# Attention stage of a hybrid encoder layer: first heads' probabilities in small buffers, stores issued ahead of the next stage's loads, cache pieces copied behind the exponential

## What is computed

```python
sc = jnp.einsum('blhd,bmhd->bhlm', qc, kb) * scale + bias
sc = jnp.where(valid, sc, -jnp.inf)
p = jax.nn.softmax(sc, axis=-1)
return jnp.einsum('bhlm,bmhd->blhd', p.astype(vb.dtype), vb)
```

## Time and profile before

| what | value |
|---|---|
| runs | 2070.66 us median of 3 (2070.57 to 2071.6) |
| the profiled execution | 2072.05 us; span 2070.3 us |
| mean granted TensorE clock | 0.975 |
| busy: TensorE, VectorE, ScalarE, GpSimd | 1951.8, 742.1, 633.8, 603.2 us |
| attention stage in the trace | from about 613 to about 822 us |

### The profile page before, as it was taken

One profiled execution on the slowest core, in us unless ns is written; L12 is line 12 of the kernel. 1 busy time (PEld: TensorE's weight loads), 2 busy tenths in 40 slices (PEclk: granted clock), 3 DMA queues, 4 the chain that ended last, 5 costly groups with the idle time before them and its releaser, 6 DMA issues. The chain is left out here.

```text
span 2070.3 us, 34075 instructions
## 1 busy us (share of the span) xinstructions
PE 1951.8 (94%) x13954; PEld 1762.3 (85%) x13954; DVE 742.1 (36%) x1467; ACT 633.8 (31%) x1239; POOL 603.2 (29%) x466
## 2 busy tenths in 40 slices
PE   5999999999995888899989999999999999999998
PEld 3999999999993566678789878999999999999996
DVE  4111577211113665465564164222222222222225
ACT  5100222100013665344353244322222222222222
POOL 6111112211122000554244344333333323333323
PEclk7999999999997999899989999999999999999999
DMA  5122222632216321231154322211111111111123
GB/s 136 59 93 86 75 93 90 233 94 90 86 61 199 117 83 38 67 104 46 30 155 145 112 92 92 58 45 41 41 41 41 46 47 41 41 41 41 41 73 151
DMA packets 159271, 169.18 MB, mean 82 GB/s; under 512 B 14187, under 2 KB 130043, under 8 KB 159150
## 3 DMA queue, kind: packets, MB, share of 16 engines
q1 hardware_dynamic: 152814, 141.52, 22.4%
q10 hardware_dynamic: 6336, 25.96, 3.1%
HBM read 126.84 MB, written 40.55 MB: 81 GB/s over the span
## 5 line engine op out<-in xcount | busy, mean ns | idle before, releaser
L2277 DVE TENSOR_TENSOR t_acc<-t_acc,t_B 128x512 f32<-128x512 f32 x252 | 173.4, 688 | 540.7 <-PE t_B L2370 540.7
L116 PE MATMUL i_ps<-x_hi,i_w_lo 128*128 128x384 f32 x1056 | 353.5, 335 | 0.0
L116 PE MATMUL i_ps<-x_hi,i_w_hi 128*128 128x384 f32 x1056 | 353.5, 335 | 0.0
L116 PE MATMUL i_ps<-x_lo,i_w_hi 128*128 128x384 f32 x1056 | 353.3, 335 | 0.0
L2357 PE MATMUL t_B<-t_merged_hi,t_wm_lo 128*128 128x384 f32 x768 | 256.9, 335 | 1.0 <-POOL t_wm_lo L1982 1.0
L2357 PE MATMUL t_B<-t_merged_lo,t_wm_hi 128*128 128x384 f32 x768 | 256.6, 334 | 0.0
L2357 PE MATMUL t_B<-t_merged_hi,t_wm_hi 128*128 128x384 f32 x768 | 256.6, 334 | 0.0
L106 POOL TENSOR_TENSOR i_w_lo<-i_w_raw,i_w_hi 128x1024 fp32r<-128x1024 f32 x44 | 104.9, 2385 | 443.8 <-ACT i_w_hi L101 443.8
L1982 POOL TENSOR_TENSOR t_wm_lo<-t_raw,t_wm_hi 128x1024 fp32r<-128x1024 f32 x49 | 119.2, 2434 | 295.6 <-ACT t_wm_hi L2057 295.6
L116 PEld LDWEIGHTS i_ps<-x_hi,i_w_lo 128*128 128x128 f32 x1056 | 198.8, 188 | 0.0
L116 PEld LDWEIGHTS i_ps<-x_lo,i_w_hi 128*128 128x128 f32 x1056 | 198.7, 188 | 0.0
(11 more groups left out here) (321 smaller groups left out, 3404.4 us busy)
## 6 DMA issues: line engine op xcount, KB each, us to landing
proj<-i_out ACTq DMA_DIRECT2D x44, 576.0 KB, 2.8
i_w_raw<-in_w_in SPq DMA_DIRECT2D x44, 512.0 KB, 3.8
t_raw<-in_w_up SPq DMA_DIRECT2D x32, 512.0 KB, 4.5
t_raw<-in_w_down SPq DMA_DIRECT2D x32, 512.0 KB, 3.6
t_gates<-proj SPq DMA_DIRECT2D x48, 192.0 KB, 2.6
a_k_cache<-in_cache_attn_k SPq DMA_DIRECT2D x8, 1024.0 KB, 5.2
a_v_cache<-in_cache_attn_v SPq DMA_DIRECT2D x8, 1024.0 KB, 5.2
d_c<-proj SPq DMA_DIRECT2D x3, 1536.0 KB, 7.2
```

The costliest lines, as they stand in the source:

```text
L116: last = pe.matmul(out, a[s][:, c, :], b[:, c, tokens], start=k == 0, stop=k == n - 1)
L2277: dve.tensor_tensor(a, a, B[(ND * j + d) % 4][:, :], ALU.add).then_inc(added, 1)
```

## The change

Three edits in `stage_attention`. First, two small buffers of 128 x 128 (`first_pt`) are put behind the exponentials' buffers, and `turned_p(u)` gives them to the units 2, 3, 6 and 7, the only heads of the first block that used `pt[2]` and `pt[3]`. Those buffers' first user is now u = 10, and the wait for the stores moves there. Second, SP issues the two conv loads after the six stores. Third, ScalarE's side jobs stand behind the exponential of their step.

```diff
-        assert late + 8 * KEYS <= env.c_at + 16 * T
+        assert late + 8 * KEYS + 8 * P <= env.c_at + 16 * T
...
+        first_pt = [nc.alloc_sbuf_tensor_at(f"a_first_p_t{i}", [P, P], F32, offset=late + 8 * KEYS + 4 * P * i) for i in range(2)]
...
+        def turned_p(u):
+
+            return first_pt[u % 4 - 2] if u < AH and u % 4 > 1 else pt[u % 4]
...
             sp.wait_ge(pre_d, (NPRE) // 2)
             sp.wait_ge(pre_a, (NPRE + 1) // 2)
-            for a, ts in ((0, TP), (P, 0)):
-                sp.dma_start(env.c0[:, :, a:a + P], env.proj[3 * AW:3 * AW + CONV, ts:ts + P].rearrange(
-                    "(c p) t -> p c t", p=P)).then_inc(env.c_in, 16)
             for h in range(AH):
...
             sp.dma_start(O_["sample_conv"].rearrange("l b w c -> (l b w) c"),
                          tail_out[HIST:ROWS, :]).then_inc(saved, 16)
+            for a, ts in ((0, TP), (P, 0)):
+                sp.dma_start(env.c0[:, :, a:a + P], env.proj[3 * AW:3 * AW + CONV, ts:ts + P].rearrange(
+                    "(c p) t -> p c t", p=P)).then_inc(env.c_in, 16)
             for b in range(2, NB):
...
-                if u == 2:
+                if u == AH + 2:
                     act.wait_ge(saved, 16 * 6)
                 if u >= 4:
                     act.wait_ge(av_made, group(u - 4) + 1)
-                act.activation(pt[u % 4][:, 0:n], TR[:, 0:n], ACT.Copy).then_inc(tr_read, 1)
+                act.activation(turned_p(u)[:, 0:n], TR[:, 0:n], ACT.Copy).then_inc(tr_read, 1)
...
             for st in range(STEPS):
                 if 0 <= st - 3 < NU:
                     turned(st - 3)
-                for j in side_jobs(st):
-                    side_out(j)
                 if st < NU:
...
                                    accum_out=rsum[:, st % SR:st % SR + 1]).then_inc(p_made, 1)
+                for j in side_jobs(st):
+                    side_out(j)
...
-                                         pt[(u + w) % 4][:, i * P:(i + 1) * P], start=i == 0, stop=i == n - 1)
+                                         turned_p(u + w)[:, i * P:(i + 1) * P], start=i == 0, stop=i == n - 1)
```

## The result

The changed kernel took 2056.77 us, the median of four runs (2055.30 to 2059.61), beside 2070.61 for the kernel before (2070.03 to 2071.60): a ratio of 0.9932, interval 0.992 to 0.9943. The forecast was 2053.9 with a range up to 2055.9, so the median lies 0.9 above the range. The profiled execution took 2055.41 with a span of 2053.7; against the 2072.05 of the one profiled before that is -16.64, where the sum said -16.8. Two repeats of the changed kernel gave 2054.26 (ratio 0.9922, 0.9902 to 0.9942) and 2056.34 (0.993, 0.9915 to 0.9945). All its 14 runs lie between 2051.86 and 2061.79 with a median of 2055.9, all 36 runs of the kernel before between 2066.57 and 2076.28 with one of 2071.5.

A forecast was written before the change was run, and what follows sets the result against it. ScalarE's wait at u=2 for the last of six late stores was taken to bound the attention opening. Terms -17.8 and +1.0 sum to -16.8, from the median 2070.66 to 2053.9 us; range 2049.0 to 2055.9.

The forecast's parts named there:

- The stall, -17.8: ScalarE's copy of u=2 no longer waits for the last of six stores and goes on at 633.23: -17.8 us.
- The moved wait, 0: ScalarE at u=10: stores done at 642.2 to 646.0, u=10 due at 649.9 or later, so no cost.
- The small fill just in time, and the hold, +1.0: GpSimd's small bias fill ends at 638.63, in time; its large fill holds VectorE's scaling of u=5: +1.0 us (0.4 to 1.6).
- The third edit, 0: Cache pieces copied behind ScalarE's exponential: no gain or loss, within 1 us either way.
- the rival of 22.6 us: Rival: the third edit pays, VectorE's waits for exponentials outside the hole go too: 2031.3 us, chance 0.08.
- The clock, 0: TensorE's clock in the attention opening: no gain taken, since stream scores now wait behind the scaling.
- the rival's -3: Rival: the clock stays up, worth about -3 us, and VectorE is not held: 2049.9 us, chance 0.22.
- u=11 near 655: Sign that the forecast is right: head u=11 in the attention stage comes near 655 us; it stood at 671.85.
- The carry to the median: Durations came from one profiled execution, 2072.05 us; the result was carried down by 1.39 to the runs' median.
- The wait at u=10: Rival: stores land at 651.02 as before and ScalarE waits at u=10 instead: 2054.0 us, chance 0.06.
- the slower case: Rival: cache copies, late by an exponential, fall on TensorE's path: up to 2080.2 us, chance 0.03.
- the case without gain: Rival: the wait is moved and nothing gained, needing stores that land at 667.68 or later: chance 0.01.

The follow-up runs named there:

- e2_loads: Kernel before plus only the second edit, the conv loads issued behind the six stores, with u=2 still waiting for them: 2062.20 us, ratio 0.9966.
- e5_pieces: Whole change with GpSimd's large bias fill cut into eight pieces, one per head: 2057.28 us in its one run.
- e3_copies: Kernel before plus only the third edit, cache pieces copied behind the exponential: 2071.78 us over ten runs, ratio 1.0005.
- e4_no_third: Whole change without its third edit, cache pieces copied ahead of the exponential as before: 2055.15 to 2058.51 us in three runs, a fourth left out.
- e11_squares: On the reordered attention, ScalarE's squares of the delta stage's first group moved ahead of that stage's first exponentials: 2055.74 us.
- reordered attention: Whole change with the large fill in eight pieces, small fill first, first stream's diagonal queries four steps earlier; also called reordered version: median 2052.6 us over ten runs.
- e9_warm: On the reordered attention, 13 products that nobody reads added on TensorE in the attention stage's opening: median 2053.52 us.
- e1_buffers: Kernel before plus only the first edit, small buffers and moved wait, conv loads still ahead of bias loads and stores: 2059.82 us, ratio 0.9942.
- e12_change_5: The whole changed kernel run again unaltered, six runs from 2051.86 to 2061.79 us, median 2056.34.
- e10_order_again: The reordered attention run again unaltered: 2054.68 us, beside 2056.34 for the change on the same chip.

## Why the prediction was off, and where it was right

**The stall, -17.8: right.** From the begin to u=2's copy 23.25 us passed before, 5.27 now: -17.98.

**The moved wait, 0: right.** u=10 waits for no store; e2_loads puts the stores' end at 643.23.

**The small fill just in time, and the hold, +1.0: right, in place and size.** The scaling ended 0.08 after the large fill, and the stream's reduction came at 639.74, within the 639.2 to 640.4 of the forecast. From the begin it moved from 28.83 to 11.69, so -17.14: 0.84 less than the stall. That the fill was the cause is shown by e5_pieces (0.42 instead of 2.34). The Trainium skill, SBUF — State Buffer, section "SBUF: two separate sides", calls the shared ports an exclusive lock for a whole instruction. The trace agrees: the scaling took 2.34 us beside a fill of 2.74, and 0.42 beside pieces of 0.51.

**The third edit, 0: right, for a reason of its own.** The argument was that the copies have room before TensorE turns; the waits show that VectorE's gain is passed on to TensorE's scores, as the text held against the rival of 22.6 us. e3_copies and e4_no_third leave nothing over.

**The clock, 0: the term that failed.** It was set at one value, with -3 as another outcome, as though the changed kernel had one clock. It has several. From the stream's reduction to the end of the stage, 166.69 us before, the three profiles of the change took 164.94, 164.94 and 167.12: -1.75, -1.75 and +0.43. A clock term of 0 meant as much time at half clock behind the reduction as before, 10.2 us; it was 6.7, 6.7 and 13.6, and with none (e11_squares) the stretch takes 163.04, so that the rival's -3 would have been -3.65. The forecast's u=11 near 655 is met by the third (655.45) and missed by the first (652.73). The delta stage, at no cost in the sum, gave +1.98, -1.55 and -1.98 in the same three, with 29.6, 19.3 and 17.5 us at half clock where it had 22.8 before. So the profiled -16.64 agreed with -16.8 by luck: 1.75 gained and 1.98 lost nearly cancelled.

**The carry to the median, and the range: what put the result outside.** The sum was made for one execution and carried down by 1.39, the distance of the profiled execution to a median of three runs that lay within 1.03 us of each other. Its ends came from the bounds of the costs, with nothing for the runs. Both kernels spread by 10 us: 2066.57 to 2076.28 before, 2051.86 to 2061.79 after. The sum for the profiled execution, 2055.25, came true (2055.41). The 2.9 us between 2053.9 and the median of four runs, 2056.77, are nearly all carry: 1.39 down for a profiled execution above its median, and 1.36 because the changed kernel's profiled execution lay below its own. The two longer of the four had mean clocks of 0.977 and 0.976, the shorter 0.979; in which stage their surplus lies stays open, as neither has a profile. Over all fourteen runs the median is 2055.9, at the range's very edge. The difference of the medians over all runs is 15.6, where the forecast had 16.8. Two bounds do not follow from the terms either: 2070.66 - 16.8 - 0.6 - 1 is 2052.3, not 2052.5, and no term gives 2055.9, where the sum's own bound is 2055.5.

**The rivals.** The wait at u=10, the slower case and the case without gain did not come. The third edit's 22.6 us did not come either (e3_copies, e4_no_third). The clock that stays up appeared in no profile of the change, only in one of the three of the reordered attention (e11_squares) and in e9_warm; what kept it up there is not shown.

## What to carry to other kernels

When a stall is taken away, look for the next thing that waits on the same queue: here the small bias loads behind the conv loads would have kept 3.8 us of the gain (e1_buffers), though the stores themselves were early enough. An edit that moves a wait from one engine to another (VectorE from exponentials to scores) was worth nothing here, since the engine waited for at the end came no earlier. And where the granted clock moves within a kernel, size a change of a few us on stretches between landmarks, with the time at half clock of each stretch beside it, and put the spread of the runs into the range.

## What the runs showed of the hardware

Not expected was how much the clock differs between executions of the same code. The reordered version's opening ran wholly at 2.4 GHz in one profile and with 20.5 and 23.9 us at 1.2 GHz in two others; the change's with 6.8, 6.8 and 13.7. The first stream's scores, one group of eight products of TensorE, took 1.06 us at 638.31 after the change, at full clock, and 1.93 before, at half clock. Of a stage, each us at half clock cost some 0.3 us (an estimate, from the two straight lines in the part on the spread). Once down, it stayed at 0.50 while TensorE was at work: 8.53 busy us of 10 in the window 640 to 650 of e12_change_5, and 8.69 at 0.56 in e10_order_again. Its fall at 631 in e10_order_again came after TensorE had waited 0.69, 0.71 and 0.63 us at its first three stops; in e11_squares the same stops took 0.69, 0.71 and 0.70, and it stayed up. What picks the execution in which it falls was not found: the begins of the reordered version's three profiles lie at 626.96, 627.54 and 627.92, and no run sets them apart on purpose.

Cutting a copy of 128x3072 on GpSimd into eight cost 4.50 - 2.74 = 1.76 us more, some 0.25 us for each of the seven added instructions, with a wait behind each.
